# Joined beginning, group norm and index unit in a kernel of two blocks: PSUM operands on VectorE, norm weights in the rotation matrices

## What is computed

```python
h = x                                                  # (1, 512, 1024)
proj = rms_norm(h, norm_mix_w) @ w_in                  # y = x * rsqrt(mean(x*x) + eps) * w
...
y = rwkv7_scan(r, decay, k, v, kk, a)                  # heads of 64; linear in v
mean = jnp.mean(y, -1, keepdims=True)
var = jnp.mean(jnp.square(y - mean), -1, keepdims=True)
y = (y - mean) * lax.rsqrt(var + GN_EPS)
y = (y * lnx_w + lnx_b + bonus) * g
...
h = h + memory_cross_attn(rms_norm(h, norm_mem_w), rms_norm(mem, norm_src_w), ...)
...
(qa, ka, va, iq, ik, iw, qb, kb, vb, g_low, og) = split(n @ w_in_ab)   # ik 64 columns, iw 8, g_low 16
qa = rope_partial(rmsnorm(qa, gq), pos)                # 4 heads of 128; ka the same with gk
iq, ik = rope_partial(iq, pos), rope_partial(ik, pos)  # 8 index heads of 64, one key head
logits = einsum('bthd,bsd->bths', iq, ik) * 64 ** -0.5
score = einsum('bths,bth->bts', relu(logits), iw * 8 ** -0.5)
idx = top_k(score, 128)                                # masked to the chunks up to the query's
oa = attention of qa over the chosen ka, va
ob = gla_chunked(qb, kb, vb, log_sigmoid(gate) / 16)   # needs exp(b_last - b) per chunk of 128 here
```

## Time and profile before

| what | value |
|---|---|
| median of three runs | 2245.12 us |
| the profiled execution, its own time | 2249.7 us |
| its span in the trace | 2247.6 us |
| TensorE busy in the span | 2141.2 us |
| VectorE busy | 927.2 us |
| ScalarE busy | 598.6 us |
| GpSimd busy | 1419.6 us |
| mean granted clock of TensorE | 0.989 of full |

### The profile page before, as it was taken

How to read it: one execution, slowest core, us unless ns; L and a number is a source line. 1 busy time by engine, 2 the same in 40 slices (tenths; PEclk the granted TensorE clock), 3 DMA queues, 4 the chain that set the end, 5 groups by cost and what they waited for, 6 DMA issues and landing times.

```text
span 2247.6 us, 32735 instructions
## 1 busy us (share of the span) xinstructions
PE 2141.2 (95%) x13158; PEld 1729.6 (77%) x13158; DVE 927.2 (41%) x1452; ACT 598.6 (27%) x1186; POOL 1419.6 (63%) x1644
## 2 busy tenths in 40 slices
PE   6998999989999999998988999999999989999999
PEld 4775788768888888776766888888877768888887
DVE  7677453623421122358996421022246554210210
ACT  3334422413220021213325321021145462200210
POOL 6963322753887777765652677777765437777774
PEclk9999999999999999999998999999999999999999
DMA  4321111321333333221220233333321213333333
GB/s 159 94 75 38 49 32 50 122 66 57 123 93 97 100 93 96 92 80 52 63 59 20 85 94 95 102 94 95 101 75 57 65 38 94 94 95 102 94 95 101
DMA packets 50817, 184.74 MB, mean 82 GB/s; under 512 B 5632, under 2 KB 5760, under 8 KB 50560
## 3 DMA queue, kind: packets, MB, share of 16 engines
q1 hardware_dynamic: 50400, 181.20, 26.3%
q10 hardware_dynamic: 288, 1.77, 0.2%
HBM read 180.85 MB, written 2.10 MB: 81 GB/s over the span
## 4 chain that ended last, share of the span: by engine, by line
PE 85%; DVE 11%; ACT 2%; issue 2%; DMA 0%; ACTq 0%; DVEq 0%; SPq 0%
PE PB L1648 23%; PE PB L1649 23%; PE PB L1651 23%; PE PB L1612 10%; DVE AR L922 4%; PE PB L2017 2%; ACT AR L446 2%; PE PB L1720 2%; PE PB L1615 1%; DVE AR L925 1%; DVE AR L1414 1%; DVE SM L1411 1%; DVE HN L925 1%; DVE AR L1457 1%; PE PB L1687 1%
## 5 line engine op out<-in xcount | busy, mean ns | idle before, releaser
L437 POOL TENSOR_TENSOR WL<-W,WH 128x256 fp32r<-128x256 f32 x1312 | 1060.7, 840 | 27.4
L1649 PE MATMUL PB<-AR_r,WL 128*128 128x512 f32 x2360 | 919.4, 390 | 0.0
L433 POOL TENSOR_SCALAR WH<-W 128x1024 fp32r<-128x1024 f32 x328 | 359.6, 1096 | 783.7 <-DMA W<-weights_in 783.6
L1651 PE MATMUL PB<-AR_r,WH 128*128 128x512 f32 x2360 | 582.9, 389 | 0.0
L1649 PEld LDWEIGHTS PB<-AR_r,WL 128*128 128x128 f32 x2360 | 443.6, 188 | 95.3 <-issue 4.6
L1651 PEld LDWEIGHTS PB<-AR_r,WH 128*128 128x128 f32 x2360 | 443.0, 188 | 91.9
L1648 PE MATMUL PB<-HN_r,WH 128*128 128x512 f32 x1184 | 473.0, 399 | 0.1
L1648 PE MATMUL PB<-AR_r,WH 128*128 128x512 f32 x1176 | 458.6, 390 | 0.0
L446 ACT ACTIVATE AR<-AR 128x512 f32<-128x512 f32 (+4 forms) x269 | 157.2, 623 | 754.4 <-DVE AR L925 670.6
L925 DVE SCALAR_TENSOR_TENSOR AR<-PB,AR 128x512 f32<-128x512 f32 (+3 forms) x153 | 99.0, 647 | 442.2 <-PE PB L1651 387.9
L922 DVE TENSOR_TENSOR H<-H,PB 128x512 f32<-128x512 f32 x80 | 55.0, 688 | 533.2 <-PE PB L1651 512.9
(11 more groups left out here) (123 smaller groups left out, 1342.1 us busy)
## 6 DMA issues: line engine op xcount, KB each, us to landing
W<-weights_in SPq DMA_DIRECT2D x328, 512.0 KB, 3.5
H<-x_in SPq DMA_DIRECT2D x8, 512.0 KB, 6.8
C<-constants_in SPq DMA_DIRECT2D x4, 512.0 KB, 4.8
h_out<-H SPq DMA_DIRECT2D x8, 256.0 KB, 4.7
H<-mem_in ACTq DMA_DIRECT2D x1, 1024.0 KB, 4.8
C<-constants_in SPq DMA_DIRECT2D x1, 736.0 KB, 11.7
V<-vectors_in ACTq DMA_DIRECT2D x1, 703.0 KB, 4.7
C<-constants_in SPq DMA_DIRECT2D x1, 68.0 KB, 3.7
```

The source lines that it names most:

```text
L433: pool.tensor_scalar(WH[:, u % RING, :], w, 1.0, 1.0, ALU.mult, ALU.mult).then_inc(sems["w_round"], 1)
L437: low = pool.tensor_tensor(WL[:, u % RING, part], w[:, part], WH[:, u % RING, part].bitcast(F32), ALU.subtract)
L1649: pe.matmul(out, ll, rh, start=False, stop=False)
L1651: ins = pe.matmul(out, lhs(k)[0], rhs(k)[0], start=False, stop=stop and k == KT - 1)
```

## The change

**Beginning.** The planes are not normalised. x_hi is x times the norm weight, rounded by ScalarE as x arrives; x_lo is one fused operation of VectorE on the same x. 1/rms (plane RS0) multiplies after the product: VectorE evicts all 26 units of the mix stage (`shift`, DQ, DK, `value_ev`) with RS0 as the second operand, instead of ScalarE's copies. Unit 0 runs by `unit_part`, three matmuls per plane; GpSimd splits it in four parts of 256 columns; the norm's sum stands behind unit 1. The order of the loads is: weights 0 behind the first constants, x pairs 0 and 1, weights 1, pairs 2 and 3, weights 2 and 3, then the rest of V and C. The small products `prep` are placed otherwise between units 14 to 17. ScalarE prepares the memory tokens in one block ahead of its other work.

**Group norm.** The value tokens are made by a product with the matrix `center` (identity minus the mean over 64), so y has mean zero; the mean's sums and subtractions go. ScalarE squares the first three chunks' columns before the last chunk is evicted. VectorE's last twelve operations are interleaved over the planes.

**Memory norm.** `norm_sum(N_MEM)` moves behind the first query unit.

**Index unit.** i_k and misc become one unit: SyncE loads 64 columns of each into one slot (misc in the lower half of each tile, i_k in the upper one). Step 5 has no unit; `rope_mm(4)` makes two products, with parts of ident and rope_i, which also bring i_k to both halves. AT counts the positions of units in the stream, which now differ from their numbers in memory.

**Index sums.** The relu stays in its PSUM bank, VectorE reads it there, and the bank is free when the multiply-add is done. RLU goes.

**Rotations.** T1 goes: the product times sin stays in PB[3]. For the heads the norm weight is multiplied into the matrix (ROPE_Q, ROPE_K) and into the cosine's operation, `rope_mm` starts on the evicted plane, and 1/rms multiplies last. `a_scale` goes.

**Others.** The 1024-column difference for exp(b_last - b) becomes eight short exponentials with a bias on ScalarE; the four masked copies of GLA's last level go to ScalarE; `topk_end` has one operation less. The order of constants follows.

The diff, cut to its core:

```diff
+    put("center", np.eye(P) - (row // 64 == col // 64) / 64.0)
...
+                if u == AT["i_k"]:
+
+                    for n, name in enumerate(("misc", "i_k")):
+                        to = W[:, u % RING, :].rearrange("p (k n) -> p k n", n=P)[:, :, 64 * n:64 * n + 64]
+                        of = w_d[UNIT[name], :, :].rearrange("p (k n) -> p k n", n=P)[:, :, 0:64]
+                        sp.dma_start(to, of).then_inc(slot_loaded[u % RING], 16)
+                    continue
...
+            for n in range(KT // 2):
+                act.wait_ge(x_in[n], 16)
+                for k in (2 * n, 2 * n + 1):
+                    f(x_hi("mix", k), H[:, k, :], ACT.Copy, scale=vec("norm_mix", k, k + 1)).then_inc(*A.inc("x_hi"))
+                if n:
+                    square_mix(n - 1)
...
+            act.wait_ge(sems["y_ev"], 6)
+            for p in range(4):
+                f(YSQ[p][:, 0:3 * P], HN[:, p, 0:3 * P], ACT.Square).then_inc(*A.inc("gn_sq"))
...
+                        f(PB[6 + n % 2][:, 0:w], PB[6 + n % 2][:, 0:w], ACT.Relu, scale=0.125).then_inc(*A.inc("idx_r"))
...
+                    for n in range(8):
+                        p, t = divmod(n, TT)
+                        f(GED[:, p, tile(t)], GB[:, p, tile(t)], ACT.Exp, scale=-1.0 / 16, bias=GLAST[:, n:n + 1])\
+                            .then_inc(*A.inc("g_ede" if n == 7 else None))
...
+                for k in (2 * n, 2 * n + 1):
+                    dve.wait_ge(sems["x_hi"], k + 1)
+                    stt(x_lo("mix", k), H[:, k, :], vec("norm_mix", k, k + 1), x_hi("mix", k).bitcast(F32), ALU.mult, ALU.subtract)\
+                        .then_inc(*D.inc("x_lo"))
+                if n:
+                    add_squares(2 * n - 2)
+                    add_squares(2 * n - 1)
...
-                dve.wait_ge(sems["ev_act"], m + 1)
                 cur = PX[:, m, 1:PW]
+                dve.wait_ge(sems["w_used"], AT["rwkv_lora"] + m + 1)
+                tt(cur, PB[m % 4][:, :], RS0, ALU.mult).then_inc(*D.inc("ev_dve"))
+                dve.wait_ge(*D.latest)
...
+            for n in range(6):
+                if n:
+                    dve.wait_ge(*D.latest)
+                if n < 4:
+                    dve.wait_ge(sems["gn_rs"], n + 1)
+                if n >= 2:
+                    tt(HN[:, n - 2, :], HN[:, n - 2, :], GT[:, n - 2, :], ALU.mult).then_inc(*D.inc("mix_out"))
+                if 1 <= n < 5:
+                    stt(HN[:, n - 1, :], HN[:, n - 1, :], vec("lnx_b", n - 1, n), BON[:, n - 1, :], ALU.add, ALU.add).then_inc(*D.inc())
+                if n < 4:
+                    stt(HN[:, n, :], HN[:, n, :], vec("lnx_w", n, n + 1), SIG[:, n, :], ALU.mult, ALU.mult).then_inc(*D.inc())
...
+            dve.wait_ge(*D.latest)
+            ts(ROPE_Q, cst("rope_a"), GQS, None, ALU.mult).then_inc(*D.inc())
+            ts(ROPE_K, cst("rope_a"), vec("gk_a"), None, ALU.mult).then_inc(*D.inc())
...
-                tt(T1, PB[3][:, :], sin, ALU.mult).then_inc(*D.inc())
-                tt(x, x, cos, ALU.mult).then_inc(*D.inc())
+                tt(PB[3][:, :], PB[3][:, :], sin, ALU.mult).then_inc(*D.inc())
+                if j >= 5:
+                    stt(x, x, GQS if j < 9 else vec("gk_a"), cos, ALU.mult, ALU.mult).then_inc(*D.inc())
+                    dve.wait_ge(*D.latest)
+                    tt(PB[3][:, :], PB[3][:, :], x, ALU.add).then_inc(*D.inc())
+                    dve.wait_ge(*D.latest)
+                    dve.wait_ge(sems["a_rs"], j - 4)
+                    tt(x, PB[3][:, :], RA[:, (j - 5) % 2, :], ALU.mult).then_inc(*D.inc("rope_ev"))
+                    return
+                tt(x, PB[2][:, :] if j == 4 else x, cos, ALU.mult).then_inc(*D.inc())
                 dve.wait_ge(*D.latest)
-                tt(x, x, T1, ALU.add).then_inc(*D.inc("rope_ev"))
+                tt(x, PB[3][:, :], x, ALU.add).then_inc(*D.inc("rope_ev"))
```

```diff
-                    ts(SCORE[:, t, 0:w], RLU[:, n % 2, 0:w], IW[:, t, h:h + 1], None, ALU.mult, None).then_inc(*D.inc("idx_acc"))
+                    ts(SCORE[:, t, 0:w], PB[6 + n % 2][:, 0:w], IW[:, t, h:h + 1], None, ALU.mult, None).then_inc(*D.inc("idx_acc"))
                 else:
                     dve.wait_ge(*D.latest)
-                    stt(SCORE[:, t, 0:w], RLU[:, n % 2, 0:w], IW[:, t, h:h + 1], SCORE[:, t, 0:w], ALU.mult, ALU.add)\
+                    stt(SCORE[:, t, 0:w], PB[6 + n % 2][:, 0:w], IW[:, t, h:h + 1], SCORE[:, t, 0:w], ALU.mult, ALU.add)\
...
-            def a_scale(j):
-
-                x = rope_plane(5 + j)
-                dve.wait_ge(sems["a_rs"], j + 1)
-                stt(x, x, GQS if j < 4 else vec("gk_a"), RA[:, j % 2, :], ALU.mult, ALU.mult).then_inc(*D.inc("a_sc"))
...
-                tt(s, s, EQ[:, 0:w], ALU.add).then_inc(*D.inc())
-                dve.wait_ge(*D.latest)
-                ts(s, s, -1.0, -NEG, ALU.add, ALU.mult).then_inc(*D.inc())
+                stt(s, EQ[:, 0:w], -NEG, s, ALU.mult, ALU.add).then_inc(*D.inc())
...
-            norm_sum(N_MIX)
...
+            unit_part(0, "mix", 0, 0, KT)
+            free[0] = ("ev_dve", 1)
+            unit[0] += 1
+            project(1, 1, "ev_dve", "mix", evbase=1)
+            norm_sum(N_MIX)
...
-                    last = tr(PB[bank][:, tile(p)], src)
+                    last = mm(PB[bank][:, tile(p)], src, cst("center")) if n == 1 else tr(PB[bank][:, tile(p)], src)
...
-                group_sum(p, HN[:, p, :], (sems["y_ev"], 8), "gn_c")
+                group_sum(p, YSQ[p], (sems["gn_sq"], 5 + p), "gn_ln")
...
-            for p in range(4):
-                group_sum(p, SIG[:, p, :], (sems["gn_sq"], p + 1), "gn_ln")
...
-            norm_sum(N_MEM)
-            project(2, 6, "mq_ev", "mem", first="unit", banks=8)
+            project(2, 6, "mq_ev", "mem", first="unit", banks=8, norm=N_MEM)
...
-                    pe.wait_ge(sems["a_sc"], j - 4)
+                    pe.wait_ge(sems["ev_dve"], EVD[QK_AT[j - 5]])
...
+                if j == 4:
+
+                    take(2)
+                    for b, name in ((2, "ident"), (3, "rope_i")):
+                        twice = cst(name, 64, P + 64)[64:P]
+                        last = mm(PB[b][:, :], twice, IK[64:P])
+                        free[b] = ("rope_ev", 5)
+                    last.then_inc(*T.inc("rope_mm"))
+                    return
+                mm(PB[3][:, :], cst("rope_i") if j < 5 else ROPE_Q if j < 9 else ROPE_K, rope_plane(j)).then_inc(*T.inc("rope_mm"))
                 free[3] = ("rope_ev", j + 1)
...
-                        free[b] = ("idx_r", n + 1)
+                        free[b] = ("idx_acc", n + 1)
```

392 lines of the change are left out of this document (184 added, 208 removed).

## The result

The changed kernel takes 2231.05 us (median of five runs, 2225.11 to 2234.76) against 2245.07 us for the kernel before (five runs, 2243.08 to 2246.34). The ratio is 0.9938, with a 95% interval of 0.992 to 0.9955: faster by 14 us, where 27.5 were forecast. The time lies just above the upper end of the range (2231.0) and within three microseconds of rival A (2228.5). Six more runs, in another job, gave 2226.62 and a ratio of 0.9935.

A forecast was written before the change was run, and what follows sets the result against it. TensorE bounds the kernel, busy 2141.2 of 2247.6 us; VectorE bounds one late stretch. Terms -16.6 +1.9 -1.6 -6.2 -5.0 sum to -27.5; from 2249.7 that is 2222.2, less 4.6 for the median, said as 2217.5; range 2204 to 2231.

The forecast's parts named there:

- rival A: Index sums cost more than VectorE gives back: 2 us more a round, stretch behind yields 5, not 8.3; 2228.5 us; chance 0.14.
- VectorE has its remainder by 15.9: Beginning: plane 7 rounded at 14.9 us, its remainder by 15.9, so unit 2 starts at 23.4, not 40.03; gain 16.6.
- My part 2: VectorE up to the first attention: 26 evictions, 17.7 us, mostly fill gaps; one place without gaps gives a 1.9 us wait.
- the wait of 1.9 us: First score product: TensorE waits for VectorE's run, which takes in four DK evictions; 1.9 us lost, bounds 0 and 5.
- The group norm's 1.6: Group norm: mean's products go, 3.5 us; value tokens made by a product cost 1.9; net gain 1.6, bounds 0 and 4.
- the held bank at 9 us: Index sums: bank held until VectorE has summed; 5 us for two waits in each round, 4 us for VectorE's work between sums.
- 8.3 and 1.1: VectorE's savings: 8.3 us in the stretch it bounds (rotations, masked copies, top-k ends), 1.1 for one subtraction moved to ScalarE.
- C: First attention: VectorE late by all nine evictions, 6 us instead of 1.9, then half pace; 2223.5 us; chance 0.10.
- B: GpSimd's weight splits bound the beginning, 5.98 us against TensorE's 5.44, 8 us over 15 units; 2225.5 us; chance 0.13.
- E: Merge and moved norm don't do what they say, since other waits end there; 2225 us; chance 0.04.
- D: Sums' two banks stop overlapping: with four units 77 us instead of 40; 2245.5 to 2256; chance 0.03 slower, 0.03 no change.
- F: PSUM operands cost what the skill's page says: 45 operations at 0.07 us more; 2220.5 us; chance 0.04.

The follow-up runs named there:

- the undone part: Group norm put back as before: on four banks (job 3) 2209.83 us, ratio 0.9839; on four banks, remainders first, keys' norm later (job 5) 2203.38 us, 0.9804.
- job 3: Here: group norm as before against index sums on four PSUM banks, 2209.83 us against 2204.51, ratios 0.9839 and 0.9819.
- job 5: Here: group norm as before against four banks with remainders first and keys' norm later, 2203.38 us against 2200.59, ratios 0.9804 and 0.9786.
- The filler matmuls: Changed kernel plus two or three idle matmuls behind each of the 24 index products, into an unread bank: 2225.42 us, ratio 0.9919.
- four banks: Changed kernel with the 24 index sums over four PSUM banks instead of two: 2205.51 us, ratio 0.9836; again 2204.51 us, 0.9819.
- Its yardstick: Changed kernel with four banks, VectorE's remainders first and keys' norm later: 2201.99, 2199.4 and 2200.59 us, ratios 0.9812, 0.9807 and 0.9786.
- the kernel with the merge back: Four banks, remainders first, keys' norm later, with i_k and misc as two units again: 2198.12 us, ratio 0.9798.
- the one with the fifth rotation moved: Four banks, remainders first, keys' norm later, with the fifth rotation's product in another bank: 2201.22 us, ratio 0.9813.

## Why the forecast was off, step by step

The difference of the two traces at the end of each place (units matched one by one; negative is earlier than before):

| place | forecast for it | trace | running difference |
|---|---|---|---|
| unit 2 ended | -16.6 | -10.9 | -10.9 |
| up to the first value unit of the attention | +1.9 | -2.3 | -13.2 |
| attention, scan, memory units, group norm | -1.6 | -8.6 | -21.9 |
| memory norm | -6.2 | -6.8 | -28.7 |
| index: merged unit up to the first sum | -2.2 | -1.5 | -30.2 |
| sums, and the stretch behind | -2.8 | +6.6 | -23.6 |

Behind that the difference stays within 0.8 us.

**What bounds it** was read rightly: the large products did not move, and each gain and loss lies at one of the five places.

**The beginning** was right in its data and weights (7.79 against 7.5) and wrong in one step: "VectorE has its remainder by 15.9". It was there at 20.2. I let VectorE's queue hold only the remainders. An addition of 1.33 us stands ahead of those of planes 4 and 5, two of 1.1 us ahead of the last two, and a remainder took up to 1.3 us, not 1.0. The slow pace that I had added for the first planes came there (0.43 us a matmul up to 10.9) and, behind the wait of 2.73 us, once more for the last planes and nine matmuls of unit 1, which took 7.2 us instead of 5.44. The experiments add what no trace of before could show: with a start that early, VectorE's backlog near 72 us costs 7.0 us. My part 2 looked for VectorE's lateness only at the first attention ("One place has none"), and it was the bank of unit 10.

**Up to the attention** the wait of 1.9 us did not come. VectorE's run had the four evictions in it, but its 24 multiplications took 22.9 us instead of 25.1. And there is a gain of 2.3 us that I had put at nothing, with the words "elsewhere the stages keep their time": the small products `prep` are not only placed otherwise. Before, the products that read partitions 0 to 63 stand ahead of those that read 64 to 127, and the 16 take 6.4 us (105.88 to 112.3). After, the two kinds take turns, each pair starts within 0.01 us (94.99 and 95.00), and the 16 take 4.0 us.

**Group norm and memory norm.** The memory norm came as worked out (6.8 in the trace, 5.8 by the ratio). The group norm's 1.6 is near the 1.8 us of the undone part where no lower clock plays in; the row shows 3.2 us at that place, and before has a stretch at the lower clock there (421.1) that after has not. The 1.11 us wait stays, as forecast (1.11 at 399.02). Its two parts were both mis-sized: the place gave 1.8 and not 3.5, and of the centring product's +1.9 nothing is seen. With transposes in its place, TensorE takes the same time from unit 27 to unit 40 within 0.1 us in job 3, and 2.0 us more in job 5, with one more stretch at the lower clock. Of the 8.6 us of that row, some 5 are, as far as the traces tell, no part of the change: the trace of before has four stretches of 3.4 us at the lower clock between 223 and 333 us, that of after one at 339, and the nine traces of kernels that share this part with after have none to three. This is why the traces lie further apart than the medians, and why it was wrong to carry the 4.6 us between before's profiled execution and its median over to the changed kernel.

**The index unit.** The wait at the fourth rotation was there as written (2.4 us forecast, 2.41 to 2.72 measured), and the merge gained 1.5 in this trace against the 2.2. The step that failed is the price of that wait: I put 2.4 us for it and nothing for the lower clock behind it, a stretch of 3.4 us that nine of the fifteen traces with this wait have behind it, once or twice, and the five traces without the wait have not. Where it is missing the merge gained 2.3 us, where it came twice it lost 1.5. The times of the whole show no gain.

**The index sums are the step that failed most.** I priced the held bank at 9 us for TensorE; it was 19.6. The four rounds took 37.3 us against 22.8, 14.5 more instead of 9; and the three units between them took 7.1 to 7.6 us instead of 5.7, 5.1 more, which I had not in the sum, since TensorE's standing brought the lower clock. Together that is 10.6 us above my price, where rival A had 8. I had the pattern in the earlier trace rows and used it only for the gain at the memory norm. The second error is in who pays: I let VectorE's end be 3.3 us later. VectorE stood 42.0 us between its first sum and the end of its stretch, against 17.5 before, since its eviction at the head of each round waits for a unit at half pace.

**VectorE's savings were larger than forecast.** Its busy time over the same stretch fell by some 17 us, not 8.3 and 1.1. Rotations (0.4 to 0.5 a head) and top-k ends are near the forecast, the four copies gave 1.4 and not 2.1, and the fused operation took 1.11 with the key's weight and 0.85 with the query's, on average the 1.00 that I took. Left out were the 24 sums themselves: with an operand in PSUM a sum of 384 columns took 0.62 us and not 0.89, one of 256 columns 0.48 and not 0.62, one of 512 columns 0.75 and not about 1.0, together about 5 us. These are also the times of the quickest sums of before, with both planes in SBUF (0.62, 0.48 and 0.75): the operand in PSUM does not make the operation cheaper, it takes away the excess of the others (up to 1.31, 1.02 and 1.58). Some 2 us more are spread over other operations. The Trainium skill (VectorE: DVE Perf Modes, The TRN2 errata) charges more for a PSUM source. The trace disagrees again: 0.69 to 0.70 for both new PSUM operations of a head. These savings, 17 us, paid for most of the 24.5 us that VectorE stood longer.

**The rivals.** A was the one that came, with its place and its mechanism, and the chance of 0.14 was too small: the row of the sums had the clearest new wait of the whole change. C did not come. B did not either, but its limit is near (the wait of 0.27 us above). E came in part: the wait at rotation four took back some of the merge, and the moved norm did what it should. D's mechanism came at about half its size: the four rounds with their units took 59.1 us, not its 77, in which D had counted four units where three stand between the rounds; alone on the kernel before it does make it slower, by 17.4 us. F did not come.

## What to carry to other kernels

Moving an operand from SBUF into PSUM frees VectorE's operation from the excess that two SBUF planes showed here while GpSimd worked, but the bank is then held by the slowest reader: count how many banks the producer needs to stay ahead (two lost 17 to 21 us here; four were some 4 us better than the old scheme, which is within the intervals). Price a new wait of TensorE in a loop with the units behind it at the lower clock, and ask which engine in turn waits for those units. A faster start is worth only what the next queue lets through: follow each engine's backlog until it first has a gap, and not only to the next known stop. Before a difference of some us between two traces is put down to an edit, look at the same place in a second execution of either kernel: one wait in this study was 17.2 and 22.2 us long in two traces of one kernel.

## What the runs showed of the hardware

- The granted clock fell to half in the rounds of the sums although TensorE was busy 51.3 of 59.1 us there. In the same place with 34.9 of 39.5 us busy it did not fall. The filler matmuls kept it at 1.00.
- Nine traces of kernels that share their first 350 us differ in which stretches of the attention and the scan run at the lower clock (none in one, three in another, most of 3.4 us). Each such stretch costs up to 1.7 us, which is the size of several terms of this forecast.
- VectorE's operations on two tensors of 128x512, in the traces of before and after together: 99 with both in SBUF beside which GpSimd ran no instruction took 0.68 to 0.70 us; those beside GpSimd's took up to 1.54, median 1.08 to 1.10 us. All 376 with one operand in PSUM took 0.67 to 0.70, with GpSimd at work or not. The Trainium skill (SBUF — State Buffer, Who interferes with whom) states that a VectorE operation with two SBUF inputs contends with GpSimd's reads and one with at most one such input, outside the two-port modes, does not; the rows of this case agree.
- Products with 64 rows ran side by side where one read partitions 0 to 63 and the next 64 to 127: eight in 1.99 us after, against 0.43 us for each that stood behind one of its own kind before.
- A stretch at the lower clock near 1150 us and one long wait there came and went between executions of the same kernel (17.2 and 22.2 us for four banks). What brings it is open.
- The kernel with the lowest ratio is before with the whole change, four banks for the sums, the remainders first, the keys' norm later and the fourth rotation in a bank of its own: 2198.45 us, ratio 0.9778 (0.9755 to 0.98). Its yardstick, the kernel with the merge back and the one with the fifth rotation moved lie within 3 us of it and can't be told from it.
- A correction to the description of the kernel before: i_k's unit does not leave 64 of its 128 columns unused, it holds its 64 columns twice, side by side. The merged unit takes them once.
